# Both heads of a pair transposed in one visit, in the sparse attention of tile 0

## The reference, cut to what matters

```python
s_s = einsum('bgrqd,bgqntd->bgrqnt', qb, k_sel) * scale
p_s = masked_softmax(s_s, mask_s)
o_s = einsum('bgrqm,bgqmd->bgrqd', p_s, v_sel)
s_w = einsum('bgrqd,bgkd->bgrqk', qb, kwb) * scale
p_w = masked_softmax(s_w, mask_w)
o_w = einsum('bgrqk,bgkd->bgrqd', p_w, vwb)
outs = stack([o_c, o_s, o_w])          # o_c: compressed branch
o = sum(gates * outs)
```

## Time and profile before

| | |
|---|---|
| runs | 2052.22, 2048.22, 2050.76 us |
| median | 2050.76 us |
| the profiled execution | 2052.06 us, its span 2050.3 us |
| busy: PE, DVE, ACT | 2018.8, 1119.0, 941.5 us |
| granted TensorE clock | 0.995 of full speed |

### The profile page before, as it was taken

How to read it: one execution, slowest core, us unless ns; L and a number is a source line. 1 busy time by engine, 2 the same in 40 slices (tenths; PEclk the granted TensorE clock), 3 DMA queues, 4 the chain that set the end, 5 groups by cost and what they waited for, 6 DMA issues and landing times.

```text
span 2050.3 us, 25732 instructions
## 1 busy us (share of the span) xinstructions
PE 2018.8 (98%) x9814; PEld 1667.8 (81%) x9814; DVE 1119.0 (55%) x1404; ACT 941.5 (46%) x1193; POOL 6.4 (0%) x16
## 2 busy tenths in 40 slices
PE   8999999999999999999998999999999999999998
PEld 6788888888888888877777788888888888888886
DVE  5454545455445555766667775644445454444444
ACT  5444444444454444455553465554444444444443
POOL 0000000000000000000001000000000000000000
PEclk9999999999999999999999999999999999999999
DMA  8666666666656557565442365566666666655554
GB/s 285 188 191 188 187 188 190 188 191 209 213 187 193 187 169 221 176 197 154 133 133 83 123 201 170 155 194 189 190 189 190 190 188 185 213 188 193 194 195 144
DMA packets 198824, 376.44 MB, mean 184 GB/s; under 512 B 13152, under 2 KB 19680, under 8 KB 198624
## 3 DMA queue, kind: packets, MB, share of 16 engines
q1 hardware_dynamic: 195984, 372.97, 59.5%
q10 hardware_dynamic: 2768, 2.48, 0.4%
HBM read 373.31 MB, written 2.10 MB: 183 GB/s over the span
## 4 chain that ended last, share of the span: by engine, by line
PE 96%; DVE 2%; ACT 1%; issue 1%; DMA 1%; SPq 0%; DVEq 0%; ACTq 0%
PE psum L1453 90%; PE psum L1476 2%; PE psum L1655 1%; PE psum L1688 1%; PE psum L1555 1%; PE psum L1465 1%; PE psum L1668 0%; PE psum L1744 0%; DVE kgT L1265 0%; DMA w_raw<-in_w_out 0%; DVE att L1276 0%; DMA w_raw<-in_g 0%; DVE qfT L1263 0%; PE psum L1634 0%; PE psum L1885 0%
## 5 line engine op out<-in xcount | busy, mean ns | idle before, releaser
L895 DVE TENSOR_TENSOR w_lo<-w_raw,w_hi 128x1024 fp32r<-128x1024 f32 x696 | 852.2, 1227 | 889.8 <-ACT w_hi L488 888.1
L488 ACT ACTIVATE w_hi<-w_raw 128x1024 fp32r<-128x1024 f32 x696 | 736.6, 1060 | 1038.5 <-PE psum L1453 1010.5
L1453 PE MATMUL psum<-w_hi,xT_hi 128*128 128x512 f32 (+1 forms) x1824 | 715.7, 392 | 10.9 <-DVE w_lo L895 9.1
L1453 PE MATMUL psum<-w_hi,xT_lo 128*128 128x512 f32 (+1 forms) x1824 | 709.3, 389 | 0.0
L1453 PE MATMUL psum<-w_lo,xT_hi 128*128 128x512 f32 (+1 forms) x1824 | 709.3, 389 | 0.0
L1453 PEld LDWEIGHTS psum<-w_hi,xT_hi 128*128 128x128 f32 x1824 | 343.6, 188 | 86.1 <-issue 16.2
L1453 PEld LDWEIGHTS psum<-w_hi,xT_lo 128*128 128x128 f32 x1824 | 343.6, 188 | 71.2
L1453 PEld LDWEIGHTS psum<-w_lo,xT_hi 128*128 128x128 f32 x1824 | 343.9, 189 | 68.5
L1453 PE MATMUL psum<-w_hi,ffT_hi 128*128 128x512 f32 x784 | 306.3, 391 | 0.0
L1453 PE MATMUL psum<-w_hi,ffT_lo 128*128 128x512 f32 x784 | 305.2, 389 | 0.0
L1453 PE MATMUL psum<-w_lo,ffT_hi 128*128 128x512 f32 x784 | 305.0, 389 | 0.0
(11 more groups left out here) (230 smaller groups left out, 868.3 us busy)
## 6 DMA issues: line engine op xcount, KB each, us to landing
w_raw<-in_g SPq DMA_DIRECT2D x176, 512.0 KB, 3.7
w_raw<-in_u SPq DMA_DIRECT2D x176, 512.0 KB, 3.6
w_raw<-in_d SPq DMA_DIRECT2D x176, 512.0 KB, 4.5
w_raw<-in_w_in SPq DMA_DIRECT2D x88, 512.0 KB, 3.7
w_raw<-in_w_out SPq DMA_DIRECT2D x32, 512.0 KB, 3.7
w_raw<-in_cw SPq DMA_DIRECT2D x8, 512.0 KB, 3.8
w_raw<-in_wk SPq DMA_DIRECT2D x8, 512.0 KB, 5.2
w_raw<-in_wq SPq DMA_DIRECT2D x8, 512.0 KB, 3.6
```

What stands on the lines that cost most here:

```text
L488: nc.scalar.activation(w_hi[:, slot], w_raw[:, slot], ACT.Copy).then_inc(w_hi_ready, 1)
L895: nc.vector.tensor_tensor(w_lo[:, slot], w_raw[:, slot], w_hi[:, slot].bitcast(F32), ALU.subtract)\
L1453: mm = nc.tensor.matmul(dst[:, t, 0:width], act_t, w[:, slot, kk, 0:width], start=(first and kk == 0 and n == 0), stop=(last and kk == KT_ ...
```

## The change

For the pairs of tile 0 (turned in iterations 2 to 9) all four transposes of a pair, two for each head, go in one visit, right behind the scores of pair i and ahead of slot(2i). P V of pair i-3 follows them. ScalarE takes the whole bank by one copy, at the head of its iteration. The semaphores count by two, so that tile 1, which is left as it was, finds the same values. Line numbers behind the new functions are shifted: the matmul of `unit` is line 1462 and that of the scores 1664.

```diff
# ScalarE
+            def take_pair(i):
+                act.wait_ge(p_turned, 2 * i + 2)
+                if i:
+                    act.wait_ge(pv_done, 2 * i)
+                nc.scalar.activation(probT[:, :, 0:2 * P], psum[:, 6, :].rearrange("p (x s) -> p x s", x=2),
+                                     ACT.Copy).then_inc(pT_ready, 2)
+
             for i in range(18):
+                if 2 <= i < 10:
+                    take_pair(i - 2)
                 slot(2 * i)
-                if i >= 2:
+                if i >= 10:
                     takeT(2 * i - 4)
...
                 slot(2 * i + 1)
-                if i >= 2:
+                if i >= 10:
                     takeT(2 * i - 3)
# TensorE
+            def turn_pair(i):
+                pe.wait_ge(p_ready, i + 1)
+                pe.wait_ge(pcT_ready, 1)
+                if i:
+                    pe.wait_ge(pT_ready, 2 * i)
+                for c in range(4):
+                    tr = nc.tensor.transpose(psum[:, 6, c * P:(c + 1) * P],
+                                             prob[i % 3][:, c // 2, (c % 2) * P:(c % 2 + 1) * P], ident[:])
+                tr.then_inc(p_turned, 2)
...
             for i in range(18):
                 if i < 16:
                     scores(i)
-                slot(2 * i)
-                if i >= 2:
-                    turn_p(2 * i - 4)
+                if 2 <= i < 10:
+                    turn_pair(i - 2)
                     if i > 2:
                         values(i - 3)
+                slot(2 * i)
+                if i >= 10:
+                    turn_p(2 * i - 4)
+                    values(i - 3)
                 slot(2 * i + 1)
-                if i >= 2:
+                if i >= 10:
                     turn_p(2 * i - 3)
```

## The result

| | before | after |
|---|---|---|
| median of 20 runs each | 2048.20 us | 2053.37 us |
| mean | 2048.74 | 2053.05 |
| lowest | 2046.89 | 2050.14 |
| the profiled execution, its span | 2052.06, 2050.3 | 2050.29, 2048.5 |

The changed kernel takes 1.0022 of the time before, 95% interval 1.0015 to 1.0028: slower by 4.5 us, at the edge of the 0.2% (4.1 us) from which the prediction counted a change. The forecast of 2053.5 agrees with the median, but by two errors that cancel: the base of three runs, 2050.76, lay 2.6 above what twenty runs give, and the difference is 4 to 5 us, not 2.7.

The account below looks back on a forecast made before the run. TensorE was taken to bound the kernel, busy throughout the changed stretch. A gain of 1.1 us from merged visits and waits of 3.8 us made +2.7 on 2050.76, so 2053.5 us, range 2050.0 to 2056.5.

Parts of the forecast that it names:

- What bounds: Tile 0's pairs, 914 to 985 us: TensorE busy throughout all 71.00 us, so only its row of starts counts.
- The waits: Transposes wait for VectorE's probabilities into iterations 3, 5, 7, 9: 0.57, 0.58, 2.49, 0.15 us, together 3.8; none elsewhere.
- The gain of the merged visit: Iterations 2 to 9: one TensorE visit replaces two, saving 0.14 us an iteration, 1.1 us for eight.
- four transposes to what follows, 0.53: Piece of the new visit's price: time in us from four transposes to the next work, taken from tile 1.
- Scores to transposes: Piece of the merged visit that no row showed: taken as 0.65 us, bounds 0.6 and 0.74.
- the 0.14 an iteration: Gain in us: two old visits cost 2.13 beyond their weight units, the new one 1.99.
- What the gain consists of: One slow return to the weight stream fewer, the size of the 0.14 us; array shape changes stay four an iteration.
- ScalarE at no cost: Two 128x256 copies become one 128x512, ending while the weight unit runs ahead of ScalarE's split: cost 0.
- The sum: Whole kernel: gain -1.1 plus waits +3.8 makes +2.7 us, so 2053.5 us.
- The rival of the clock: The 2.49 us wait before iteration 7 halves TensorE's clock for the next unit, adding 2.8 us: 2056.3; chance 0.14.
- The base: Median of three runs of the kernel before, 2050.76 us, to which the forecast change was added.
- The chances: Whole kernel against a 0.2% (4.1 us) bound: same 0.69, slower 0.28, faster 0.03.

Follow-up runs that it names:

- experiment 4: Kernel before, with only weigh(i-1) put ahead of slot(2i) on VectorE for i = 1 to 8; one execution, 2048.76 us, attention stretch 88.76 us.
- experiment 2: Changed kernel with weigh(i-1) ahead of slot(2i) on VectorE for the first eight pairs; median 2048.5 us, ratio to before 0.9996.
- experiment 3: Changed kernel with only weigh(5), the pair of the long wait, put early on VectorE; median 2049.79 us, ratio to before 1.0002.
- experiment 5: Changed kernel with the first eight weighs early, and take_o(0) ahead of slot(12) on VectorE and ScalarE; median 2048.79 us, ratio to before 0.9999.
- experiment 7: As experiment 5, with the merged visit turned round: transposes and P V first, scores last; median 2047.85 us, ratio to before 0.9995.
- Experiment 6: Changed kernel with joint transposes, P V and the one copy moved behind slot(2i), so two visits remain; median 2049.03 us, ratio to before 1.0002.
- experiment 8: Changed kernel with six unused VectorE additions ahead of weigh(5), lengthening the long wait; five executions, median 2056.47 us, ratio to before 1.0039.
- experiment 9: Changed kernel with pair 7's scores computed four times over, filling most of the long wait; median 2052.25 us, ratio to before 1.0021.
- experiment 1: The changed kernel again, unchanged, twice in two comparisons on two chips; medians 2053.45 and 2053.51 us, ratios to before 1.0019 and 1.0022.

## Why the prediction came out as it did, point by point

- **What bounds.** Right. TensorE's starts carried everything: the stretch of every kernel is that of before plus waits and steps on TensorE, to 0.1 us, where the clock stayed up. That VectorE alone can't win anything is what the one trace of experiment 4 shows.
- **The waits.** Right, and the strongest part: 0.57, 0.58, 2.49 and 0.15 were worked out, 0.57, 0.57, 2.48 and 0.15 measured (the last from 991.39 to 992.61, less 1.07), 3.77 in place of 3.79; none in 4, 6 and 8. Experiments 2 and 3 undid them and the time went with them.
- **The gain of the merged visit.** Forecast too large: 0.7 us was measured in place of 1.1. The mis-sized term is the piece "four transposes to what follows, 0.53". It came from tile 1, where the transposes follow a matmul of the same shape; behind the scores they take 945.36 - 944.77 = 0.59. Scores to transposes, the piece that no row showed, was 0.65 as taken. The visit with its unit is 948.58 - 943.80 = 4.78 and not 4.71, which leaves 0.07 of the 0.14 an iteration, against 0.09 by experiment 5. That this price comes with the scores in front is shown by experiment 7, where the same transposes ahead of the scores take 0.53 again.
- **What the gain consists of.** Right: one return to the stream fewer. Experiment 6, with two visits and all else of the change, has none of it. The runs show two costs, about 0.1 us at the return and 0.06 to 0.09 at the scores' changes of shape, so the order within a visit counts too. The Trainium skill (TensorEngine Tiling (Array Packing), Key Properties) says that a change of tiling mode drains TensorE. The runs agree that such a change costs something, but by that rule alone experiment 5 would show no gain, and it shows 0.72 us.
- **ScalarE at no cost.** Right. Its one copy waits 3.92 us for TensorE's P V in iteration 7, in time in which ScalarE had nothing else, and no wait of TensorE in the stretch names it.
- **The sum.** 3.77 - 0.69 = 3.08 us in the trace where 2.7 was forecast. The lowest runs say the same, over three comparisons: 3.25, 3.40 and 2.79 above the lowest of before, 3.15 on average. That the total of 2053.5 met the median of 2053.37 was luck: the base was 2.6 too high, and the medians differ by 5.2 in place of 2.7.
- **The rival of the clock.** It was a case beside the forecast, with 0.14. It is a part of it: one profiled execution of three of the changed kernel had it, with 2.82 us, and so had experiment 8. The error was to ask whether the wait lowers the clock, as if the answer were the same for each execution. It would be enough for the missing 4.3 - 3.1 = 1.2 us if it came in about four of ten executions (1.2 / 2.82). That this is where the 1.2 us come from isn't shown: experiment 9 took most of the wait away and left the mean where it was, and experiment 3 took it away, with the two signs told there. In experiment 5, without any wait in the stretch, 4 of 11 executions had 0.995 or less; in experiment 2, none of 11. A rival of the same size stands ahead of the stretch, in code that the change doesn't touch. From the first matmul on kcT to scores(0) seven of the twelve traces take 15.22 us; the other five (before, and experiments 3, 4, 7 and 9) have a fall of the clock there and take 16.8 or 18.4 us. Whether the change makes that fall more frequent wasn't tested.
- **The base.** The three runs of before scatter by 4 us, and their median was 2.6 too high. Their lowest, 2048.22, lay at the median of twenty. This error was as large as the whole forecast change, and alone it hides the errors of the sum.
- **The chances.** No change, by 4.1 us, had 0.69 and slower 0.28. The ratio's interval, 1.0015 to 1.0028, lies across this bound, a little more of it above. Base aside, the traces put the difference at 3.1 us with the clock up in the stretch and at 5.9 with the fall of experiment 1.
- **Left open.** What decides whether the clock falls behind the same 2.41 us wait, and what makes up the last microsecond of the means. Single executions of the changed kernel differ by up to 6.7 us among its first twenty, with mean clocks from 0.993 to 0.996. In the twelve traces what lies behind scores(10) takes 1046.0 to 1046.8 us, and what lies ahead of scores(0) 910.2 to 914.9: the scatter comes from ahead of the stretch and from within it.

## What to carry to other kernels

When work is moved ahead on the engine that never waits, measure the producer's finish from the instruction that releases it, and do the same for the new demand; here the waits then came out to 0.01 us, and the place with an extra job in front (here the group's end and take_o) is the one that costs most. Merging two visits of the busy stream was worth about 0.1 us each here, and it needs its inputs that much earlier: move the producer with it, and look for what else reads or frees the same bank. Where a change is worth 0.2%, take the base from many runs, and compare traces by a stretch between two instructions, not by their spans.

## What the runs showed of the hardware

- The same code with the same 2.41 us wait of TensorE between busy stretches was followed by a granted clock of 1.00 in two executions and of 0.50 (1.2 GHz) for 6 us in a third, at a price of 2.82 us; in the one trace with a wait of 5.17 us the clock fell to 0.50 as well, and its mean over the following two microseconds was 0.71. A wait of 1.85 us up to 57.06 was followed by 0.53 at 60 to 62 us in the kernel before, and by 1.00 in experiment 2, with a wait of 1.8 at that place.
- The clock also fell where TensorE doesn't wait: in five of twelve traces, between 898 and 906 us, during or right behind the compressed branch's 64 short matmuls on kcT. In the kernel before TensorE waits for nothing from 880 to 915 us. From the first of those matmuls to scores(0) it took 15.22 us with the clock at 1.00 and up to 18.42 with the fall, 3.2 more.
- Four 128 x 128 transposes take 0.53 us to the P V behind them when they follow matmuls of the full array, and 0.59 when they follow matmuls of 64 rows; a unit's last matmul is followed in 0.23 us by transposes and in 0.32 by the 64-row scores.
